# Layer 0's cache pages in groups of four over six ring slots in the order of release, and half of the index-key transfers on GpSimd's queue

## The reference, cut to what matters

```python
# layer 0: 8 heads x 2 components of 64; the past is gathered by page_table
k_all = concatenate([gather(cache_a_k), k]); v_all = concatenate([gather(cache_a_v), v])
p = softmax(where(mask, einsum('bqhcd,bkhcd->bhcqk', q, k_all) * 64 ** -0.5, -inf))
o = einsum('bhqk,bkhe->bqhe', p[:, :, 0] - lam * p[:, :, 1], v_all)
y = rms_norm(o) @ a_w_out
# layer 1: an index key of 64 per position, the top 256 of the summed relu scores are attended
dots = einsum('bqhd,bkd->bqhk', qi, concatenate([gather(cache_b_kidx), ki]))
score = einsum('bqh,bqhk->bqk', wi * idx_scale, relu(dots))
# after each mixer: x = LN(a*x + mixer(x)); x = LN(a*x + moe(x)); x = x + sigmoid(x Wg + bg) * (p Wp)
```

## Time and profile before

| | us |
|---|---|
| three runs, median (lowest to highest) | 1365.01 (1361.35 to 1365.46) |
| the profiled execution: its time | 1363.73 |
| its span, first to last instruction | 1361.9 |
| PE busy / DVE / ACT / POOL in the span | 1196.2 / 475.4 / 340.0 / 47.3 |

### The profile page before, as it was taken

The page is one execution under the profiler, slowest core; times in us unless marked ns, Lnnn a source line. Parts: engine busy times, 40 slices in busy tenths (PEclk is TensorE's granted clock), DMA queues, the critical chain, the costliest instruction groups (busy, mean ns, idle before and its releaser), DMA issues.

```text
span 1361.9 us, 19003 instructions
## 1 busy us (share of the span) xinstructions
PE 1196.2 (88%) x6635; PEld 597.6 (44%) x6636; DVE 475.4 (35%) x1035; ACT 340.0 (25%) x773; POOL 47.3 (3%) x81
## 2 busy tenths in 40 slices
PE   7999998988859999999498798998939999999856
PEld 3445666554423333333246445555433333333333
DVE  1011655552531011111534598365261111111263
ACT  1112545452102111211112414654011111211110
POOL 1200000001000000000100000000100000000101
PEclk9999999998869999999799899999958999999978
DMA  9935699979309799999531744335624989999721
GB/s 331 359 139 186 234 383 360 384 293 384 141 16 376 308 393 429 425 422 420 162 122 32 254 120 136 101 100 226 264 94 191 389 314 428 424 424 425 283 74 39
DMA packets 97278, 360.29 MB, mean 265 GB/s; under 512 B 17024, under 2 KB 35488, under 8 KB 75952
## 3 DMA queue, kind: packets, MB, share of 16 engines
q1 hardware_dynamic: 88528, 328.79, 62.2%
q0 software_dynamic: 5984, 21.59, 4.8%
q10 hardware_dynamic: 2688, 8.91, 1.7%
HBM read 341.48 MB, written 17.78 MB: 264 GB/s over the span
## 4 chain that ended last, share of the span: by engine, by line
PE 68%; DVE 9%; DMA 9%; SPq 7%; issue 4%; ACT 3%; DVEq 0%; POOL 0%; POOLq 0%; ACTq 0%
PE PS L874 15%; PE PS L597 13%; PE PS L895 8%; PE PS L847 7%; PE PS L1022 4%; DMA ring<-in_moe_w_up 3%; SPq L360 3%; DMA ring<-in_cache_a_k 3%; PE PS L1003 3%; PE PS L722 3%; SPq L449 2%; PE PS L856 2%; PE PS L884 1%; PE PS L672 1%; PE PS L877 1%
## 5 line engine op out<-in xcount | busy, mean ns | idle before, releaser
L874 PE MATMUL PS<-ring,QKV 128*64 128x512 f32 (+1 forms) x512 | 231.1, 600 | 6.6 <-ACT QKV L1336 3.9
L877 PE MATMUL PS<-ring,QKV 128*64 128x512 f32 (+1 forms) x512 | 231.0, 600 | 0.0
L1336 ACT ACTIVATE QKV<-PS 128x512 f32<-128x512 f32 (+5 forms) x180 | 95.0, 528 | 399.3 <-PE PS L847 110.0
L597 PE MATMUL PS<-ring,XT 128*64 128x256 f32 (+1 forms) x576 | 150.1, 482 | 3.2 <-DMA ring<-in_a_w_in 2.6
L874 PEld LDWEIGHTS PS<-ring,QKV 128*64 128x64 f32 (+1 forms) x512 | 71.7, 142 | 152.3 <-issue 148.2
L895 PE MATMUL PS<-ring,QKV 128*64 128x512 f32 (+1 forms) x512 | 123.8, 599 | 0.0
L847 PE MATMUL PS<-X,QKV 128*64 128x512 f32 x432 | 103.7, 616 | 15.7 <-issue 15.7
L597 PEld LDWEIGHTS PS<-ring,XT 128*64 128x64 f32 (+1 forms) x576 | 71.0, 162 | 82.4 <-issue 72.3
L2005 DVE TENSOR_TENSOR QKV<-QKV,PS 64x512 f32<-64x512 f32 (+1 forms) x32 | 21.7, 679 | 233.6 <-ACT QKV L1511 233.6
L2010 DVE COPY QKV<-PS 64x512 f32<-64x512 f32 (+1 forms) x32 | 22.2, 692 | 189.2 <-PE PS L895 189.2
L1003 PE MATMUL PS<-ring,XT 128*128 128x512 f32 (+1 forms) x256 | 74.2, 504 | 7.7 <-ACT XT L1336 7.7
(11 more groups left out here) (311 smaller groups left out, 1301.3 us busy)
## 6 DMA issues: line engine op xcount, KB each, us to landing
ring<-in_moe_w_gate SPq DMA_DIRECT2D x32, 2048.0 KB, 11.8
ring<-in_moe_w_up SPq DMA_DIRECT2D x32, 2048.0 KB, 16.1
ring<-in_moe_w_down SPq DMA_DIRECT2D x32, 2048.0 KB, 13.8
ring<-in_cache_a_k SPq DMA_DIRECT2D x64, 512.0 KB, 7.2
ring<-in_cache_a_v SPq DMA_DIRECT2D x64, 512.0 KB, 6.6
ring<-in_a_w_in SPq DMA_DIRECT2D x5, 2048.0 KB, 25.6
ring<-in_ple_gate_w SPq DMA_DIRECT2D x4, 2048.0 KB, 13.2
ring<-in_cache_b_k SPq DMA_DIRECT2D x64, 128.0 KB, 2.0
```

Source lines behind the costliest of these rows:

```text
L597: ins = pe.matmul(PS[p0:p1, banks[u % 4], 0:c1 - c0], rows_of(k, t), wt[:, k, c0:c1], start=(k == 0), stop=(k == KD - 1))
L874: ins = pe.matmul(PS[0:m, 0, :], XE[:, k, 0:m], wg[:, k, :], start=(k == 0), stop=(k == KD - 1))
L877: ins = pe.matmul(PS[p1:p1 + m, 1, :], XE[:, k, 0:m], wu[:, k, :], start=(k == 0), stop=(k == KD - 1))
L1336: ins = act.activation(dst, src, ACT.Copy) if scale is None else \
```

## The change

A page group is now four pages of one sequence, keys or values, 2 MiB, which is one ring slot. A list `LOADS` gives the order in which the 32 groups are loaded, and `page_groups` gives each of them the slot of the group that is released at that turn; the order of release is that of PE's program: of each batch the two value halves of the sequence before, then the two key halves. The first six groups take the slots as the six column chunks of `a_w_in` are used.

```diff
+LOADS = [("k", 1, 1), ("k", 0, 1), ("k", 1, 0), ("v", 0, 0), ("k", 0, 0), ("v", 0, 1), ("k", 2, 0)]
+for _b in range(1, DB):
+    LOADS += [("v", _b, 0), ("v", _b, 1)] + [("k", _b + 1, 1)] * (_b + 1 < DB) + [("k", _b + 2, 0)] * (_b + 2 < DB)
+def freed(what, b, g):
+    return ("score_mm", 3 * b + g + 1) if what == "k" else ("pv_mm", 2 * b + g + 1)
+def page_groups():
+    used = [(what, b - (what == "v"), g) for b in range(DB + 1) for what in "vk" for g in range(2)
+            if 0 <= b - (what == "v") < DB]
+    slot, load, last, count = {}, {}, {}, [0] * SLOTS
+    for i, group in enumerate(LOADS):
+        s = i if i < SLOTS else slot[used[i - SLOTS]]
+        count[s] += 1
+        slot[group], load[group], last[s] = s, count[s], group
+    return slot, load, [freed(*group) for group in used], [freed(*last[s]) for s in range(SLOTS)]
@@ SP
+            for i, (what, b, g) in enumerate(LOADS):
+                cache = cache_a_k if what == "k" else cache_a_v
+                s = group_slot[what, b, g]
+                for j in range(4 * g, 4 * g + 4):
+                    pg = page_id(b, j)
+                    if j == 4 * g and i < SLOTS:
+                        sp.wait_ge(*at("qkv_mm0", 3 * i + 3))
+                    elif j == 4 * g:
+                        sp.wait_ge(*at(*group_freed[i - SLOTS]))
+                    sp.dma_start(page(what, b, j), cache[0, bass.ds(pg, 1)]...).then_inc(pages_landed[s], 16)
-            sp.wait_ge(*at("score_mm", 3 * (DB - 1) + 2))
             for j in range(2):
+                sp.wait_ge(*at(*slot_freed[j]))
                 columns(("a_out", j), a_w_out[0], 512 * j, 512 * j + 512, False)
@@ SP, layer 1
-                    for b in range(DB):
+                    for b in range(DB // 2):
@@ GpSimd
+            pool.wait_ge(*at("page_table_landed", 16))
             pool.wait_ge(*at("or_cleared", 1))
@@ GpSimd, behind the gathers of layer 0's experts
+                    n, s = item("kidx")
+                    pool.wait_ge(*at(stream.used[n - SLOTS][0], stream.used[n - SLOTS][1]))
+                    for b in range(DB // 2, DB):
+                        for j in range(NPAGE):
+                            pg = pool.value_load(pt_sb[0:1, bass.ds(b * NPAGE + j, 1)], ...)
+                            pool.dma_start(kx[:, b // 2, j, b % 2, :], cache_b_kidx[0, bass.ds(pg, 1)]...)\
+                                .then_inc(S("late_keys_landed"), 16)
                     a, n = CONST["newmask"]
                     pool.dma_start(C[:, a:a + n], spread_c).then_inc(S("spread_landed"), 16)
@@ PE
 def page_turn(b, j):
-                pe.wait_ge(k_landed[j], b * 16 + 16)
+                if j % 4 == 0:
+                    pe.wait_ge(pages_landed[group_slot["k", b, j // 4]], 64 * group_load["k", b, j // 4])
 def past_values(b, first, last):
-                pe.wait_ge(v_landed[b % 2], 128 * (b // 2 + 1))
+                g = first // 4
+                pe.wait_ge(pages_landed[group_slot["v", b, g]], 64 * group_load["v", b, g])
-                if last == NPAGE + 1:
-                    ins.then_inc(S("pv_mm"), 1)
+                ins.then_inc(S("pv_mm"), 1)
 def batch_a(b):
-                    past_values(b - 1, 0, 5)
+                    past_values(b - 1, 0, 4)
                 scores1()
-                    past_values(b - 1, 5, NPAGE + 1)
+                    past_values(b - 1, 4, NPAGE + 1)
@@ PE, ahead of kidx_turn
             pe.wait_ge(landed[s_kidx], stream.landed[n_kidx])
+            pe.wait_ge(*at("late_keys_landed", 16 * DB // 2 * NPAGE))
```

More of the change, by code:

```diff
@@ L190, in plan @@
                 s.add(("b_in", j), ("qkv_mm1", 5 + j))
-            s.add("kidx", ("sis_mm", 9), DB * NPAGE)
+            s.add("kidx", ("sis_mm", 9), DB // 2 * NPAGE)
             for j in range(2, 5):
@@ L324, in build, with page @@
         landed = [S(f"ring_landed{s}") for s in range(SLOTS)]
[L325 to L328, removed]
+        pages_landed = [S(f"pages_landed{s}") for s in range(SLOTS)]
+        group_slot, group_load, group_freed, slot_freed = page_groups()
+        def page(what, b, j):
+            s = group_slot[what, b, j // 4]
+            return ring[:, s, :].rearrange("p (j n) -> p j n", j=4)[:, j % 4, :]
         y_p, y_s, nak_p, nav_p, nbk_p, nbv_p, nbi_p, nak_s, nav_s, nbk_s, nbv_s, nbi_s = outs
@@ L372, in _ @@
             sp.wait_ge(*at("page_table_landed", 16))
[L375 to L405, removed]
-            sp.wait_ge(*at("score_mm", 3 * (DB - 1) + 2))
+            for i, (what, b, g) in enumerate(LOADS):
[7 more added lines that the diff above has]
+                        sp.wait_ge(*at(*group_freed[i - SLOTS]))
+                    sp.dma_start(page(what, b, j), cache[0, bass.ds(pg, 1)].rearrange("a p h d -> (a p) (h d)"))\
+                      .then_inc(pages_landed[s], 16)
             for j in range(2):
+                sp.wait_ge(*at(*slot_freed[j]))
                 columns(("a_out", j), a_w_out[0], 512 * j, 512 * j + 512, False)
@@ L428, in _ @@
                     before = layer == 0 and n < 6
-                    expert(j // 3, j, (lambda j=j: sp.wait_ge(*at("pv_mm", DB - 1 if j < 2 else DB))) if before else
+                    expert(j // 3, j, (lambda n=n: sp.wait_ge(*at(*slot_freed[n]))) if before else
                            (lambda n=n: sp.wait_ge(*at(stream.used[n][0], stream.used[n][1]))))
@@ L672, in page_turn @@
                         ins = pe.transpose(PS[:, (2 * j + half) % 4, k * 128:(k + 1) * 128],
-                                           kpage[:, j, (4 * half + k) * 128:(4 * half + k + 1) * 128], ident)
+                                           page("k", b, j)[:, (4 * half + k) * 128:(4 * half + k + 1) * 128], ident)
                     ins.then_inc(S("kt_page_mm"), 1)
             def past_scores(b, g):
+                keys = ring[:, group_slot["k", b, g], :].rearrange("p (j n) -> p j n", j=4)
                 for evac in ("kt_evac_act", "kt_evac_dve"):
@@ L685, in past_scores @@
                         ins = pe.matmul(PS[32 * t:32 * t + 32, 4 + g, :], QBA[:, b, h, :],
-                                        kpage[:, 4 * g:4 * g + 4, h * 128:h * 128 + 128],
+                                        keys[:, :, h * 128:h * 128 + 128],
                                         start=(half == 0), stop=(half == 1))
@@ L719, in past_values @@
                     for t in range(4):
-                        v = vpage[:, (b % 2) * NPAGE + j, 256 * t:256 * t + 256] if j < NPAGE else \
+                        v = page("v", b, j)[:, 256 * t:256 * t + 256] if j < NPAGE else \
                             QKV[0:NS, 2, 2 * D + 256 * t:2 * D + 256 * t + 256]
@@ L764, in _ @@
             weights_turn(DB - 1)
-            past_values(DB - 1, 0, NPAGE + 1)
+            past_values(DB - 1, 0, 4)
+            past_values(DB - 1, 4, NPAGE + 1)
             fold(DB - 1)
@@ L1393, in copy_page @@
                 act.wait_ge(*at("kt_page_mm", 16 * b + 2 * j + 1))
-                copy(kpage[:, j, 0:512], PS[:, (2 * j) % 4, :], "kt_evac_act")
+                copy(page("k", b, j)[:, 0:512], PS[:, (2 * j) % 4, :], "kt_evac_act")
             def past_weights(b):
@@ L1808, in copy_page @@
                 ve.wait_ge(*at("kt_page_mm", 16 * b + 2 * j + 2))
-                ve.tensor_copy(kpage[:, j, 512:1024], PS[:, (2 * j + 1) % 4, :]).then_inc(S("kt_evac_dve"), 1)
+                ve.tensor_copy(page("k", b, j)[:, 512:1024], PS[:, (2 * j + 1) % 4, :]).then_inc(S("kt_evac_dve"), 1)
             def row_maximum(b):
```

8 lines of the change are left out of this document (6 added, 2 removed).

## The result

| | kernel before | changed kernel |
|---|---|---|
| median of the runs, us | 1365.24 (4 runs, 1361.35 to 1366.53) | 1347.72 (4 runs, 1347.36 to 1350.03) |
| the profiled execution, us | 1363.73 | 1350.03 |
| its span, us | 1361.9 | 1348.4 |

The ratio is 0.988, 95% interval 0.9857 to 0.9903: 17.5 us faster, where 22 were forecast. The changed kernel ran twice more beside other kernels, with 0.9884 (0.9864 to 0.9904) and 0.9911 (0.9893 to 0.9928), so 12 to 17.5 us is what the three comparisons give.

The account below looks back on a forecast made before the run. PE bounds the kernel nearly everywhere, so only its idle or low-clock time can be regained: -11.8 (attention) - 10.3 (index keys) = -22.1, from the median 1365.01 giving 1342.9, stated as 1342; forecast 1337 to 1346, range 1336 to 1354.

Parts of the forecast that it names:

- the 1348 of the rival: Attention: transfers stay the bound, so PE's waits for pages shrink by only 5.7 us; 1348 us, chance 0.08.
- Attention, -11.8: Layer 0's attention: PE's twelve waits for key pages vanish, 20.5 us a batch instead of 22.49; -11.8 us.
- The reason given for the lead: Attention: slots come free in PE's order, a batch (20.5 us) before need for the tightest groups, leaving 8.9 us.
- The limit of 358 GB/s: Attention: the skill's HBM limit would make a batch 23.4 us and the term some -3; the prediction rejected it.
- The reply from the earlier trace: Against that limit: five slices in the layer's experts ran at 420 to 429 GB/s.
- Index keys, -8.6 - 1.7: Start of layer 1: PE's pause for index keys goes, -8.6 us, and the slow-clock transposes behind it, -1.7.
- the bounds of 0.75 to 2.6: GpSimd's time per index-key page in us, lower and upper end; 1.37 was taken.
- The lock by VectorE: Index keys: VectorE operations hold up GpSimd's 32 issues; at 3.5 us a page 1383 us, chance 0.05.
- The prediction's counterexample: Against the VectorE lock: GpSimd's issue at 740.44 took 0.56 us inside a DVE run from 740.26 to 741.42.
- A semaphore counts once more, which I put at nothing: Attention, PE's own program: the cut moves by one page and a semaphore counts once more; cost nothing.
- GpSimd's half counted only up to its landing: Index keys: GpSimd's 32 pages from 664.47, issued by 708, landed by 717, before PE's need at 746.66.

Follow-up runs that it names:

- the page groups alone: The changed kernel with all 64 index-key pages back on SP's queue, page groups kept: 1356.24 us, ratio 0.9955 to the kernel before.
- the order alone: Kernel before, fixed slots kept; from batch 2 SP loads four key pages, then four value pages, twice, instead of alternating page by page: 1352.17 us, ratio 0.9923.

## Why the prediction was right, and what it missed

The direction and the range held; the sum was 4.6 us too large by the medians (22.1 against 17.5). The 1347.72 lies outside the 1337 to 1346 that the forecast itself was given and beside the 1348 of the rival whose mechanism, a wait for pages in the attention, did not occur; that the range held it owes to the room made for the rivals.

- *Attention, -11.8.* The mechanism held: no wait for pages, 20.66 us a batch against the 20.5 foreseen, 405 to 407 GB/s, which is all that this pace asks for. It gave 10.0 us in this profile and 10.3 in that of the page groups alone. About 1.1 us went to the waits for ScalarE's softmax. The reason given for the lead, free slots in the order of release, was not needed; the order alone did as much, so that the term came out does not speak for its reason.
- *The limit of 358 GB/s.* The Trainium skill's figure in "DMA: Bandwidth & Descriptors", section Specifications, did not hold: 405 to 407 GB/s over whole batches. The reply from the earlier trace rows was right, though the row has four slices in each layer's experts at 420 or more, not five.
- *Index keys, -8.6 - 1.7.* Right in both parts: the pause of 8.56 us is gone (8.4 us in this profile, 6.6 to 9.0 in the others, the spread of the third column), and 1.67 us of slow transposes. GpSimd took 1.135 us a page, inside the bounds of 0.75 to 2.6 and under the 1.37 chosen. The issue was the 0.54 to 0.56 of the earlier trace rows, but a sum of issue and read is not what sets the pace: the reads stand 1.13 to 1.14 us apart even where the issues follow each other by 0.53.
- *The lock by VectorE.* Its cost did not come, but its mechanism shows. One issue took 0.93 us in place of 0.54, and it stands beside this operation of VectorE:

```profile
665.89 0.93 POOL L543 DMA_DIRECT2D ring<-in_cache_b_kidx  x1 [0.60 <-issue]
```
```profile
665.89 0.81 DVE L1925 TENSOR_SCALAR X<-X,small 128x1024 f32<-128x1024 f32 x1
```

The issue ended 0.118 us behind that operation. In the nine profiles with index keys on GpSimd nine issues took 0.67 to 1.03 us, and each ended 0.117 to 0.124 us behind a TENSOR_SCALAR of this kind. Issues that had begun over 0.1 us ahead of one, or would have ended later than it anyway, were not held, and issues beside SCALAR_TENSOR_TENSOR, or TENSOR_TENSOR as at 740.44, took 0.54 to 0.61. A held issue lost at most 0.49 us, and the whole was no longer for it: all seven profiles with 32 pages took 32.6 to 32.7 us from the first issue to the end of the last, the two without a held issue too. The prediction's counterexample was thus the wrong kind of operation; the rival cost nothing because the operations that hold an issue are short and few here.
- *"A semaphore counts once more, which I put at nothing."* This is the first step that failed: the edits to PE's own program were given no cost. Fewer waits make that program shorter, the taken branch's code moved, and the entry of the experts became 2.4 to 3.3 us longer.
- *GpSimd's half counted only up to its landing.* The second step that failed: 32 transfers more made the drain at the very end 2.6 us longer, on the path that sets the end. No row of the prediction looked at the end of the program.

Together these are 5.0 to 5.9 us against a shortfall of 4.6 in the medians. In the profiled execution it is 8.4 (13.7 gained): 5.0 from these two, 1.8 from the attention, and of the last 1.6 us 1.5 can be placed at layer 1's entry, in that execution alone.

## What to carry to other kernels

Where waits for a stream of transfers come twice a period, look first at the order of the issues before rebuilding where they land: here five lines of order shortened the attention as much as the rebuild with free slots. Count for an edit also what it does to the length of each engine's program ahead of a taken branch, and to the end of the program; a stretch of the profile that should not have changed and did is where to look. Work given to an idle engine can cost at that engine's end, even where it is hidden in the middle.

## What the runs showed of the hardware that was not expected

- GpSimd's drain at the end takes 0.082 us for each transfer that it issued, from 65 to 109 of them ((8.97 - 5.38) / 44), whatever their size, since four stores for sixteen of the same bytes saved 0.98, and whether or not a read of the page table goes with them, since index keys and stores give the same slope. At 141 it is 9.54, where the rule would give 11.6. Why it flattens stays open.
- Fifteen instructions that are never executed made the kernel's entry into the experts 2.9 us shorter, by moving the code behind them.
- Two executions of the same code differ by 1 to 2 us in a stretch with the granted clock as the only difference seen: in two profiles of the changed kernel layer 1's experts took 252.92 us at a mean clock of 0.98 and 250.62 at 0.99; in their first 30 us the clock was 0.86 and 0.95.
- A TENSOR_SCALAR of VectorE on 128x1024 float32 held a transfer's issue on GpSimd until 0.12 us behind its own end, nine times over the nine profiles with index keys on GpSimd; TENSOR_TENSOR and SCALAR_TENSOR_TENSOR did not.
